# S5 layer: which engine makes the 32 operator stacks, when, and where they wait

## The reference, cut

```
def s5_scan(u, abar, bbar, cmat, h0):
    def step(h, u_blk):
        bu = jnp.einsum('btgn,gpn->btgp', u_blk.astype(jnp.complex64), bbar)
        bu = bu.at[:, 0].add(abar[None] * h)
        a = jnp.broadcast_to(abar, bu.shape)
        _, hs = lax.associative_scan(_linrec_combine, (a, bu), axis=1)
        y = jnp.einsum('btgp,gnp->btgn', hs, cmat).real
        return hs[:, -1], y
```

## Time and profile before

| what | value |
|---|---|
| median of 3 runs | 2633.34 us (2630.73 to 2639.4) |
| profiled execution, own time | 2635.93 us |
| its span | 2634.1 us |
| TensorE busy | 2220.4 us, 84% |
| VectorE busy | 1362.2 us, 52% |
| ScalarE busy | 906.9 us, 34% |
| GpSimd busy | 501.3 us, 19% |
| granted TensorE clock, mean | 0.906 of full |

### The profile page before, as it was taken

The page is one execution under the profiler, slowest core; times in us unless marked ns, Lnnn a source line. Parts: engine busy times, 40 slices in busy tenths (PEclk is TensorE's granted clock), DMA queues, the critical chain, the costliest instruction groups (busy, mean ns, idle before and its releaser), DMA issues.

```text
span 2634.1 us, 33814 instructions
## 1 busy us (share of the span) xinstructions
PE 2220.4 (84%) x13593; PEld 1674.5 (64%) x13593; DVE 1362.2 (52%) x2527; ACT 906.9 (34%) x1779; POOL 501.3 (19%) x457
## 2 busy tenths in 40 slices
PE   6878888779899775489788987879999977976998
PEld 5756666558556575389553443668888745545998
DVE  4648677553446999165334355453333223455554
ACT  3335454551212432154212344232222222344443
POOL 0047787311058950000000010000000000000000
PEclk8989999999899987699889987989999978887999
DMA  8254454793344329975322211223323442102553
GB/s 277 92 166 134 133 168 132 231 294 111 128 108 107 84 67 192 235 197 165 110 78 64 80 65 49 64 64 96 96 84 91 146 142 64 65 1 86 178 176 106
DMA packets 423666, 324.38 MB, mean 123 GB/s; under 512 B 65086, under 2 KB 411470, under 8 KB 422358
## 3 DMA queue, kind: packets, MB, share of 16 engines
q1 hardware_dynamic: 386452, 295.70, 38.7%
q10 hardware_dynamic: 34242, 16.92, 2.2%
q0 software_dynamic: 2816, 9.60, 1.1%
HBM read 292.42 MB, written 29.75 MB: 122 GB/s over the span
## 4 chain that ended last, share of the span: by engine, by line
PE 60%; DVE 14%; POOL 10%; DMA 6%; ACT 5%; issue 4%; SPq 1%; ACTq 1%; DVEq 0%; POOLq 0%
PE ps L119 58%; POOL A L88 9%; DVE A L88 3%; ACT A L115 3%; DMA wbuf<-ctab 2%; DVE R L88 2%; DVE A L102 2%; PE ps L122 2%; DVE A L105 1%; DVE A L92 1%; SPq L125 1%; DVE A L93 1%; POOL A L125 1%; DVE A L96 1%; DMA wbuf<-in_ada_w 1%
## 5 line engine op out<-in xcount | busy, mean ns | idle before, releaser
L119 PE MATMUL ps<-R,R 128*128 128x256 f32 (+1 forms) x3968 | 843.8, 335 | 42.6 <-ACT R L115 32.5
L119 PEld LDWEIGHTS ps<-R,R 128*128 128x128 f32 x3968 | 631.9, 194 | 125.5 <-ACT R L115 26.5
L119 PE MATMUL ps<-HR,R 128*128 128x512 f32 (+1 forms) x1984 | 562.4, 368 | 44.4 <-DVE R L88 33.2
L88 DVE TENSOR_TENSOR R<-wbuf,R 128x1024 fp32r<-128x1024 f32 (+2 forms) x304 | 333.0, 1104 | 367.6 <-ACT R L115 367.5
L119 PEld LDWEIGHTS ps<-HR,R 128*128 128x128 f32 x1984 | 354.0, 191 | 110.6 <-issue 43.9
L115 ACT ACTIVATE A<-ps 128x512 f32<-128x512 f32 (+4 forms) x400 | 210.2, 555 | 598.2 <-PE ps L119 422.1
L88 POOL TENSOR_TENSOR A<-A 128x512 f32<-128x512 f32 (+3 forms) x258 | 293.5, 1152 | 568.2 <-DVE A L96 304.3
L88 DVE TENSOR_TENSOR A<-A 128x128 f32<-128x128 f32 (+4 forms) x796 | 361.9, 485 | 63.3 <-ACT A L115 26.7
L115 ACT ACTIVATE R<-wbuf 128x1024 fp32r<-128x1024 f32 (+2 forms) x304 | 270.1, 894 | 293.8 <-PE ps L119 265.7
L119 PE MATMUL ps<-H,wbuf 128*128 128x512 f32 (+2 forms) x928 | 344.1, 530 | 22.1 <-DVE H L93 22.1
L119 PE MATMUL ps<-A 128*128 128x64 f32 (+10 forms) x1736 | 295.7, 371 | 31.1 <-DMA wbuf<-ctab 10.6
(11 more groups left out here) (102 smaller groups left out, 1628.2 us busy)
## 6 DMA issues: line engine op xcount, KB each, us to landing
wbuf<-in_w_ada SPq DMA_DIRECT2D x48, 1024.0 KB, 6.8
wbuf<-in_ada_w SPq DMA_DIRECT2D x24, 1024.0 KB, 8.9
wbuf<-in_w_out SPq DMA_DIRECT2D x24, 1024.0 KB, 5.6
wbuf<-in_w_ffn_gate SPq DMA_DIRECT2D x22, 1024.0 KB, 5.4
wbuf<-in_w_ffn_up SPq DMA_DIRECT2D x22, 1024.0 KB, 5.4
wbuf<-in_w_ffn_down SPq DMA_DIRECT2D x32, 704.0 KB, 4.6
wbuf<-in_attn_w_in SPq DMA_DIRECT2D x20, 1024.0 KB, 7.0
ctab<-A ACTq DMA_DIRECT2D x64, 256.0 KB, 3.0
```

Source lines behind the costliest of these rows:

```text
L88: return self.op(lambda e: e.tensor_tensor(out, a, b, op))
L119: return self.op(lambda e: e.matmul(out, lhsT, rhs, start=start, stop=stop, skip_group_check=True))
```

## The change

The stacks leave `S5.flow`. GpSimd makes all 32 in one piece of its program, `SS.stacks`, put behind mark ln1 in the text but ahead of Mod2; what it waits for first is the mark at1 (the end of the attention), so it can begin when OUT1 begins. Each stack is written to a DRAM tensor `bstab` (512 KB, a DMA on GpSimd's queue, issued in the middle of the next stack). A stack now waits for the landing of the store of stack u-3, not for TensorE. At u = 14 GpSimd also waits for ("h2", 7), the last instruction of Mod2 on VectorE. SP loads the stacks back (`back`) into 13 other buffers: eight for u below 16, and for the later ones five that lie over BS and P, for which SP waits at u = 16 until the stores of stacks 29, 30 and 31 have landed. TensorE's `turn` waits for the loaded stack.

```
@@ flow
             e.mark("ln1")
+            if e.name == "pool":
+                SS.stacks(e)
             on(Mod2())
@@ class S5
+        self.BL = [A[:, a:a + 1024] for a in [26368 + 1024 * i for i in range(8)] + [5376, 6400, 7424, 2816, 3840]]
+    def spill_stack(self, pool, u):
+        pool.wait_ge(self.pool_step, ("st", u))
+        pool.dma(self.bstab[u], self.BS[u % 3]).then_inc(self.l_bs[u % 3], u)
+
+    def stacks(self, pool):
+
+        pool.wait_mark("at1")
...
+            if u < 31:
+                self.load_bb(pool, u + 1)
+            pool.wait_ge(self.l_pp, "p")
+            pool.wait_ge(self.l_bb[u % 2], u)
+            if u > 2:
+                pool.wait_ge(self.l_bs[u % 3], u - 3)
+            if u == 14:
+                pool.wait_ge(self.dve_step, ("h2", 7))
+            if u:
+                pool.wait_own()
+            pool.tt(BR, pw(0), bv(0), MUL).then_inc(s)
+            pool.tt(U1, pw(1), bv(1), MUL).then_inc(s)
+            t = pool.own
+            if u:
+                self.spill_stack(pool, u - 1)
+            pool.wait_for(t)
+            pool.tt(BR, BR, U1, SUB).then_inc(s)
+            t = pool.own
+            pool.tt(BI, pw(0), bv(1), MUL).then_inc(s)
+            pool.wait_for(t)
+            pool.tt(U1, pw(1), bv(0), MUL).then_inc(s)
+            pool.wait_own()
+            pool.tt(BI, BI, U1, ADD).then_inc(s, ("st", u))
+        self.spill_stack(pool, 31)
+
+    def slot(self, u):
+        return u % 8 if u < 16 else 8 + (u - 16) % 5
+
+    def back_sp(self, sp, u):
+
         if u == 0:
...
+            sp.wait_mark("ln1")
+        if u == 16:
+            for v in (29, 30, 31):
+                sp.wait_ge(self.l_bs[v % 3], v)
+        elif u >= 8 and u < 16:
+            sp.wait_ge(self.tr_done, ("bt", u - 8))
+        elif u > 20:
+            sp.wait_ge(self.tr_done, ("bt", u - 5))
+        sp.wait_ge(self.l_bs[u % 3], u)
+        sp.dma(self.BL[self.slot(u)], self.bstab[u]).then_inc(self.l_bl[self.slot(u)], u)
 
     def turn_pe(self, pe, u):
-        pe.wait_ge(*self.stacked(u))
+        pe.wait_ge(self.l_bl[self.slot(u)], u)
@@ S5.flow
             for i in (u, u + 1):
-                if i + 3 < 32:
-                    part("stack", i + 3)
+                if i + 4 < 32:
+                    part("back", i + 4)
                 part("enter", i)
...
-        for u in range(3):
-            part("stack", u)
...
         ahead(0)
         ahead(1)
+        for u in range(4):
+            part("back", u)
         u = 0
```

More of the change, by code:

```diff
@@ L1278, in __init__ @@
         self.btab = dram("btab", 128, 128, 32).rearrange("g p f -> p g f")
+        self.bstab = dram("bstab", 32, 128, 1024)
         self.kf, self.xs = dram("kf", 128, 16, 240), dram("xs", 128, 4096)
@@ L1302, in __init__ @@
         self.BB = [A[:, 5120 + 128 * i:5248 + 128 * i].rearrange("p (g r n) -> p g r n", g=4, r=2) for i in range(2)]
-        self.BS = [[A[:, 5376 + 1024 * i + 512 * r:5888 + 1024 * i + 512 * r].rearrange("p (g j n) -> p g j n", g=4, j=8)
-                    for r in range(2)] for i in range(3)]
+        self.BS = [A[:, 5376 + 1024 * i:6400 + 1024 * i] for i in range(3)]
+        self.BL = [A[:, a:a + 1024] for a in [26368 + 1024 * i for i in range(8)] + [5376, 6400, 7424, 2816, 3840]]
         self.U1 = A[:, 8448:8960].rearrange("p (g j n) -> p g j n", g=4, j=8)
-        self.U1D = A[:, 26368:26880].rearrange("p (g j n) -> p g j n", g=4, j=8)
         self.BM = [A[:, 8960 + 1024 * i:9984 + 1024 * i].rearrange("p (r g q) -> p r g q", r=2, g=4) for i in range(3)]
@@ L1317, in __init__ @@
         self.l_p, self.l_u = [[sig(f"landed_s5_{x}{i}") for i in range(n)] for x, n in (("p", 2), ("u", 4))]
+        self.l_bs = [sig(f"landed_stack{i}") for i in range(3)]
+        self.l_bl = [sig(f"landed_stack_back{i}") for i in range(13)]
         W = I["s5_w_in"][0]
@@ L1360, in ship_sp @@
             sp.dma(self.US[q][s * 16:s * 16 + 16, 16 * i:16 * i + 16, :], src[s]).then_inc(self.l_u[q], b)
[L1363 to L1367, removed]
     def load_bb(self, pool, u):
-        if u == 0:
[L1372 to L1415, removed]
@@ new lines, in load_bb, with pw, bv @@
+        if u > 1:
+            pool.wait_ge(self.pool_step, ("st", u - 2))
+        pool.dma(self.BB[u % 2].rearrange("p g r n -> p g (r n)"), self.btab[:, 4 * u:4 * u + 4, :]).then_inc(self.l_bb[u % 2], u)
+    def spill_stack(self, pool, u):
[3 more added lines that the diff above has]
+        pool.wait_mark("at1")
+        pool.wait_ge(self.l_pt, "p")
+        pool.wait_ge(self.l_bt, 1)
+        pool.dma(self.P, self.ptab[:, 0:2304]).then_inc(self.l_pp, "p")
+        pool.dma(self.SA, self.ptab[:, 2560:3072].rearrange("p (x r g) -> p x r g", x=2, r=2)).then_inc(self.l_pp, "p")
+        self.load_bb(pool, 0)
+        for u in range(32):
+            BR, BI = [self.BS[u % 3][:, 512 * r:512 * r + 512].rearrange("p (g j n) -> p g j n", g=4, j=8) for r in range(2)]
+            U1, s = self.U1, self.pool_step
+            def pw(r):
+                a = self.P[:, 1152 * r:1152 * r + 1152].rearrange("p (k g) -> p g k", k=9)[:, 4 * u:4 * u + 4, 7::-1]
+                return a.unsqueeze(3).to_broadcast([128, 4, 8, 16])
+            def bv(r):
+                return self.BB[u % 2][:, :, r, :].unsqueeze(2).to_broadcast([128, 4, 8, 16])
+            if u < 31:
[22 more added lines that the diff above has]
+        self.spill_stack(pool, 31)
@@ L1421, in turn_pe @@
             for g in range(4):
-                x = pe.tr(p[:, g * 128:g * 128 + 128], flat(self.BS[u % 3][r][:, g]), self.ident)
+                a = 512 * r + 128 * g
+                x = pe.tr(p[:, g * 128:g * 128 + 128], self.BL[self.slot(u)][:, a:a + 128], self.ident)
         x.then_inc(self.tr_done, ("bt", u))
@@ L1603, in flow @@
     def flow(self, e, on, backlog):
-        own = {("ship", "sp"): self.ship_sp, ("stack", "pool"): self.stack, ("stack", "dve"): self.stack,
+        own = {("ship", "sp"): self.ship_sp, ("back", "sp"): self.back_sp,
                ("turn", "pe"): self.turn_pe, ("turn", "act"): self.turn_act, ("enter", "pe"): self.enter_pe,
@@ L1668, in flow @@
         part("leave", 3)
-def flat(a):
-    return a.rearrange("p j n -> p (j n)")
 class Setup:
```

## The result

The changed kernel takes 2642.85 us, the median of 20 runs (2638.0 to 2651.55), against 2636.37 of 20 runs of the kernel before: ratio 1.0025, 95% interval [1.0014, 1.0036], so 6.5 us or 3.7 to 9.5 slower. The sign is certain, the size is just inside the 0.3% that was to count as no difference. The profiled execution took 2644.87 us, its span is 2643.1, 9.0 above that of before.

A forecast was written before the change was run, and what follows sets the result against it. TensorE was taken as the bound up to u = 15, then late stacks. Turn(16) at 894.8 plus 85.4 and 2 gave 982.2, 14.0 us later than 968.2; so 2647 us against 2633.3, range 2629 to 2668.

The forecast's parts named there:

- the win of the late stacks: TensorE from u = 16 on: stacks that come late cost 39.9 us, the most the change can win there.
- The norm, 8 us: VectorE's LN1 end and Mod2 beside GpSimd: 8 meetings of 0.98 us make everything behind 8 us late.
- The fourteen: GpSimd's stacks ahead of the norm: end at 712 us at the earliest, some 720 to 730 likely; projection costed at nothing.
- The eighteen, 157.3 us: GpSimd's stacks behind Mod2: 18 of 8.74 us from 729.2, the last made at 886.5.
- Store and load, 8.3 us: Wait before turn(16): 3.3 store, 3.7 load, 1.3 issues and semaphores after the last stack; turn(16) starts at 894.8.
- The halves, 85.4 + 2: TensorE from turn(16) to z's rest: four halves 48.6, four with z tile 36.8, plus 2 us for the clock.
- rival A: GpSimd through early, last stack before 872.5: 10.7 us won, 2622.6; chance 0.09 in full, 0.17 in part (no difference).
- Behind z, nothing: Leave stage: hangs on z tiles and panel loads, so all moves along with TensorE and the earlier recurrence wins nothing.
- B: Rival: norm slowed in full, 24 instead of 8 us, the fourteen ending 10 later than it; 26 more, 2673; chance 0.13.
- C: Rival: store lands in 9.1 us and shipping on SP's queue makes enter(20) wait 5; 11 more, 2658; chance 0.15.
- same: Whole kernel: time within 0.3% of 2633.3, that is 2625.4 to 2641.2 us; chance 0.17.
- slower: Whole kernel: time slower by more than the 0.3% counted as no difference; chance 0.74.

The follow-up runs named there:

- e3: The changed kernel with stacks 16 and 17 loaded into buffers of their own and the wait for the last three stores moved to stack 18; 2628.69 us.
- e4: The changed kernel with stacks 26 to 31 not made and copies of 18 to 23 loaded in their place (leaves out work); 2602.78 us.
- e2: The changed kernel with GpSimd's wait for (h2, 7) put ahead of stack 12 instead of 14; 2647.96 us.
- e1: The changed kernel without GpSimd's wait for (h2, 7) ahead of stack 14; 2642.99 us.

## Why the prediction was right, step by step

The forecast was 14 us slower; measured 6.5, and 8.7 at the point for which the sum was made, the start of z's rest. Right in sign and mechanism, too large in size (1.6 times at that point, twice in the medians): the win of the late stacks is real, and one wait at u = 16, with the longer norm ahead of it, gives back more. e3 and e4 show that the time hangs on this wait: moved by one half it costs 12.1 us less, and without it 38 are won. e2 shows that the late start of half 0 is not to blame by itself: with the norm's full time back the wait grew to 55.87 us and the time by 7.2. No part of the loss was seen behind the input half.

- **The norm, 8 us.** It took 10.1 more, begun 1.3 us earlier (the sum of squares ahead of it took TensorE 7.70 us instead of 9.39, on another clock), so Mod2 ends 8.8 later. The size was right by luck. Only three of the eight pairs and none of H's 16 met GpSimd, not eight meetings of 0.98 us; single instructions lost up to 3.6. The step failed in its price: the recurrence's average of the earlier trace rows does not carry over to another pattern. (The 20 and 76 "steps" read there are instructions, four to a step; the price is per instruction and not touched by it.)
- **The fourteen** ended at 718.6, inside my 712 to 730; the projection was hardly slowed (382 matmuls in 89.49 us, before 88.62). The reason given for costing it at nothing was misread, though: TensorE has no slack there, it runs these matmuls without a gap. The slack is VectorE's, busy for 28.6 of the 93 us from 587 to 680 before and for 40.2 in the change, and it was enough.
- **The eighteen, 157.3 us**: 883.6 - 730.15 = 153.5. The term was 3.8 too large, because a stack takes 8.59 and not 8.74 us, the store's issue 0.60 and not 0.66, and the first needs no bbar issue any more.
- **Store and load, 8.3 us**: 891.78 - 883.6 = 8.2. The store's median to landing was 3.9 us, a load's 7.8 over all, many of them beside other transfers; the one that counts was quick (issued at 887.84, landed by 891.78).
- **The halves, 85.4 + 2**: 976.87 - 891.78 = 85.1. A z half takes 8.73 us, not 9.2, as its parts overlap by 0.49; this was rival A's number. The cold clock cost 1.6 us, in the first transposes alone (3.53 us instead of 1.92; TensorE had no work from 853.2 on, and the granted clock was 0.54 on average from 853 to 866 and 0.50 from 866 to 880, the 1.2 GHz level).
- **Behind z, nothing**: 8.65 and 8.50 us, as said. recur(1) ended at 1045 instead of 1060 and won nothing.

These make 14 + 0.8 - 3.8 - 0.1 - 2.3 = 8.6. Between the 9.0 of the two spans and the 6.5 of the medians lies what single executions differ by.

Rival A needed stack 31 by 872.5 and got it at 883.6. B did not come with the pause; without it (e1) its mechanism came, and far stronger: Mod2 alone cost 29 us. C did not come. The measured +0.25% lies inside the 0.3% that was called "same", the case with a chance of 0.17, and not in "slower" with 0.74, although by its interval it is a loss. The chances were too sure of more than 0.3%: the two large errors of the sum, 3.8 us for the eighteen stacks and 2.3 for the halves, pointed the same way, and they were enough to reach "no difference" by that bound.

The Trainium skill, SBUF — State Buffer, "Who interferes with whom", says that a GpSimd instruction and a VectorE one that needs the port pair they share (two inputs in SBUF, or a two-port mode) exclude each other, the one blocked until the other ends. The trace agrees that they do, but here VectorE waited longer: 4.28 us instead of 0.69, so through about three instructions of GpSimd (5.07 us for four). The measurement decides. The same page's warning on GpSimd's DMAs beside VectorE's two-port instructions (620 ns grown to 3100, in the section "A bandwidth-pool intuition that's wrong (but worth ruling out)") would make a store in the norm's time 2.5 us longer, an estimate from these figures. No run here shows such a stall: each store was issued in 0.60 us, and in e1 those issued at 730, inside the norm, and at 757 and 765, beside Mod2's TENSOR_SCALARs, landed in 2.9 to 3.0 us, as the one at 783 did with VectorE silent (3.0).

## To carry to other kernels

Ask of work moved ahead when its **last** piece is ready and what waits for that one: reused buffers can make the first consumer of a group wait for the last producer, and moving the two first pieces elsewhere was worth one whole period of the consumer. Price a meeting of GpSimd and VectorE by the gaps in GpSimd's stream, and not by an average taken from another pattern. And stop shifting work off an engine where it is idle: two stacks back on VectorE, in its idle 35 us, gave the fastest complete version, at 2613.52 us 23.3 below the kernel before; a third was too many and gave 18.4 of them back.

## What had not been expected of the hardware

- In these traces VectorE gets its turn beside GpSimd where GpSimd's stream has a gap. In the change the TENSOR_TENSOR at 713.21 took 4.28 us beside a row of four GpSimd instructions (5.07 us) and TENSOR_SCALAR ones took up to 2.67; it ended at 717.5, and GpSimd waits for itself ahead of the fourth of these, at about 713.5 + 3 x 1.27 = 717.3 (an estimate from the row's mean); without a pause Mod2's instructions took 2.14 us each on average instead of 0.33 (34.24 and 5.25 us for 16). With a wait of GpSimd for itself before each instruction none took over 1.94. How short a gap may be is open: the TENSOR_TENSOR of 713.21 is recorded as begun 0.33 us before GpSimd's row of four, while GpSimd issued a DMA, and still waited.
- In the recurrence, beside GpSimd's stacks, VectorE's instructions took 1.4 us each in the change (10 in 14 us), 1.0 in the kernel before, 0.26 alone. That this is the same effect is argued and not tested.
- A 64 KB load on GpSimd's queue landed in 4.7 us (median) instead of 2.8 to 3.3 when it was issued right behind a 512 KB store on that queue.
